# Dilated attention of the second block by head pairs, one step behind each half chunk of the input projection

## The reference, cut to what matters

```
proj = h @ w_in                                  # 512 x 1024 by 1024 x 3088 columns
mq, mk, mv, mo, mg, aq, ak, av = split(proj)
gates = mg + gate_bias
hm = bidirectional_mlstm(mq, mk * 64**-0.5, mv, gates...)     # 4 heads, both directions
hm = rms_norm(hm, g_mh) * sigmoid(mo)
qa = partial_rope(rms_norm(aq per head, g_q), pos) * 64**-0.5  # 8 heads of 64
ka = partial_rope(rms_norm(ak per head, g_k), pos)
ha = dilated_attention(qa, ka, av)               # three windows, dilations 1, 4, 16
return concat([hm, ha]) @ w_out
```

## Time and profile before

| | before |
|---|---|
| median of three runs | 3217.79 us |
| span of the profiled execution | 3213.4 us |
| TensorE busy | 3123.6 us, 97% |
| VectorE busy | 1911.2 us, 59% |
| ScalarE busy | 1046.4 us, 33% |
| mean granted TensorE clock | 0.985 |

### The profile page before, as it was taken

The page is one execution under the profiler, slowest core; times in us unless marked ns, Lnnn a source line. Parts: engine busy times, 40 slices in busy tenths (PEclk is TensorE's granted clock), DMA queues, the critical chain, the costliest instruction groups (busy, mean ns, idle before and its releaser), DMA issues.

```text
span 3213.4 us, 37101 instructions
## 1 busy us (share of the span) xinstructions
PE 3123.6 (97%) x15003; PEld 2512.4 (78%) x15014; DVE 1911.2 (59%) x2753; ACT 1046.4 (33%) x1516; POOL 10.2 (0%) x23
## 2 busy tenths in 40 slices
PE   8999999998899999999999999999999998899998
PEld 7888888776678888788877888788887764578887
DVE  7876555645675554766657554566665565574444
ACT  4212222335442222422235222332224444442222
POOL 0000000000000000000000000000000000000000
PEclk9999999999999999999999999999999999899999
DMA  6433332210033443256532443235551220133231
GB/s 231 141 118 127 147 126 81 68 46 11 2 132 127 158 153 131 79 192 214 196 107 79 150 158 138 79 118 202 185 189 59 78 59 1 47 119 104 92 99 53
DMA packets 102996, 369.21 MB, mean 115 GB/s; under 512 B 11374, under 2 KB 12670, under 8 KB 102572
## 3 DMA queue, kind: packets, MB, share of 16 engines
q1 hardware_dynamic: 101788, 362.14, 33.0%
q0 software_dynamic: 1040, 4.71, 0.4%
HBM read 364.71 MB, written 2.10 MB: 114 GB/s over the span
## 4 chain that ended last, share of the span: by engine, by line
PE 88%; DVE 7%; ACT 3%; issue 1%; DMA 1%; SPq 0%; POOL 0%; DVEq 0%; ACTq 0%; POOLq 0%
PE ps L192 25%; PE ps L194 25%; PE ps L193 25%; PE ps L196 4%; PE ps L197 2%; DVE SQ L614 1%; PE ps L499 1%; DVE WL L184 1%; DVE HL L603 1%; DVE XT L1037 1%; DVE RAW L1499 0%; PE ps L2888 0%; PE ps L2858 0%; PE ps L2788 0%; PE ps L2555 0%
## 5 line engine op out<-in xcount | busy, mean ns | idle before, releaser
L192 PE MATMUL ps<-HH,WH 128*128 128x512 f32 x2400 | 945.3, 394 | 4.0 <-ACT S L914 2.2
L194 PE MATMUL ps<-HH,WL 128*128 128x512 f32 x2400 | 935.1, 390 | 0.0
L193 PE MATMUL ps<-HL,WH 128*128 128x512 f32 x2400 | 934.5, 389 | 0.0
L179 ACT ACTIVATE WH<-RAW 128x1024 fp32r<-128x1024 f32 x456 | 459.2, 1048 | 632.0 <-PE ps L194 361.8
L184 DVE TENSOR_TENSOR WL<-RAW,WH 128x1024 fp32r<-128x1024 f32 x456 | 542.8, 1220 | 73.5 <-ACT WH L179 73.2
L192 PEld LDWEIGHTS ps<-HH,WH 128*128 128x128 f32 x2400 | 450.7, 188 | 107.5 <-issue 9.5
L193 PEld LDWEIGHTS ps<-HL,WH 128*128 128x128 f32 x2400 | 450.9, 188 | 95.2 <-issue 3.8
L194 PEld LDWEIGHTS ps<-HH,WL 128*128 128x128 f32 x2400 | 450.5, 188 | 95.4
L1037 DVE SCALAR_TENSOR_TENSOR XT<-ps,DER,XT 128x512 f32<-128x512 f32 x512 | 346.6, 683 | 246.6 <-PE ps L194 231.8
L192 PE MATMUL ps<-GH,WH 128*128 128x512 f32 x1056 | 414.1, 392 | 4.8 <-DVE GL L945 4.8
L194 PE MATMUL ps<-GH,WL 128*128 128x512 f32 x1056 | 411.2, 389 | 0.0
(11 more groups left out here) (382 smaller groups left out, 2627.0 us busy)
## 6 DMA issues: line engine op xcount, KB each, us to landing
RAW<-in_w_modt SPq DMA_DIRECT2D x200, 512.0 KB, 5.0
RAW<-in_ffn_wi SPq DMA_DIRECT2D x182, 512.0 KB, 5.0
RAW<-in_w_gu SPq DMA_DIRECT2D x90, 512.0 KB, 4.5
RAW<-in_ffn_wo SPq DMA_DIRECT2D x88, 512.0 KB, 4.6
RAW<-in_w_in SPq DMA_DIRECT2D x44, 512.0 KB, 3.6
RAW<-in_w_down SPq DMA_DIRECT2D x44, 512.0 KB, 4.2
RAW<-in_w_out SPq DMA_DIRECT2D x16, 512.0 KB, 4.5
STG<-in_w_modt SPq DMA_DIRECT2D x10, 512.0 KB, 12.7
```

The costliest lines, as they stand in the source:

```text
L179: act.e.activation(u.hi, u.ld.view, ACT.Copy).then_inc(u.hi_done.sem, 1)
L192: pe.e.matmul(out, wh, x[0], start=first, stop=False)
L193: pe.e.matmul(out, wh, x[1], start=False, stop=False)
L194: m = pe.e.matmul(out, wl, x[0], start=False, stop=last)
```

## The change

1. The alternation of units and attention is gone. `projection` takes a function `between`; a chunk's 24 matmuls are emitted as two halves, and the function is called after the first half and after the evacuation of the chunk. Each call takes one step of the attention.
2. The attention runs head pair by head pair: j outside, n inside. A pair now has two steps: the score of this pair and the first transpose group of the last one; then the second group, the value product of the pair before it, and the counts. A step waits in the list until the norm of its head pair has been emitted. The probabilities live in freed places of the weight ring.
3. The chunks are ordered DQ, DK, DV and one other, four times over, then MV, MQ, MK, MO. Chunks use banks 0 and 1, followers banks 2 and 3 (before: four each).
4. The norm is taken on 8 numbers per token: four matmuls with the square as the stationary operand and two columns of ones moving give a 128x8 sum; logarithm and exponential give the inverse root, three small VectorE operations refine it, and eight matmuls with a broadcast column spread it over the 64 partitions of its head. One part more per follower.
5. The eight spreads of the mLSTM's maxima move from the projection to the start of the mLSTM; the sigmoids of MO move from its evacuation to behind the last unit.
6. The quotient is written per head pair, and the high and low parts of chunks 4 to 7 are made beside the first units, not after the last quotient.

The core of the diff:

```
-            st["root"] = pr.sidefree[self.b] = s["nr_act"].next()
-            st["inv"] = s["rope"].next()
-            st["scaled"] = tiles.rsfree = s["rope"].next()
+            self.ln, st["root"] = s["nr_act"].next(), s["nr_act"].next()
+            self.prod, self.half, st["inv"] = (s["rope"].next() for _ in range(3))
+            pr.sidefree[self.b] = self.prod
...
-            pe.e.matmul(P.banks[self.b], ti.PR[:, 128:256], ti.SQ, start=True, stop=True).then_inc(st["sum"].sem, 1)
+            for n in range(4):
+                m = pe.e.matmul(P.banks[self.b][:, 2 * n:2 * n + 2], ti.SQ[:, n * 128:(n + 1) * 128], ti.PR[:, 128:256:64],
+                                start=True, stop=True)
+            m.then_inc(st["sum"].sem, 1)
         elif self.part == 2:
+            pe.wait_ge(*st["inv"])
+            pe.wait_ge(*self.free)
+            for n in range(4):
+                for h in range(2):
+                    rs = ti.RS[:, st["at"], 2 * n + h:2 * n + h + 1].broadcast_to([128, 64])
+                    m = pe.e.matmul(P.banks[self.b][64 * h:64 * h + 64, n * 128:(n + 1) * 128], rs, P.ID, start=True,
+                                    stop=True, skip_group_check=True)
...
-            act.e.activation(ti.RS, P.banks[self.b], ACT.Sqrt, scale=1.0 / 64, bias=P.EPSC).then_inc(st["root"].sem, 1)
+            act.e.activation(r, P.banks[self.b][:, 0:8], ACT.Ln, scale=1.0 / 64, bias=P.EPSC).then_inc(self.ln.sem, 1)
+            act.wait_ge(*self.ln)
+            act.e.activation(r, r, ACT.Exp, scale=-0.5).then_inc(st["root"].sem, 1)
...
+class MlSigmoid(Step):
...
+        for h in range(4):
+            act.e.activation(m.O[:, h, :], m.O[:, h, :], ACT.Sigmoid).then_inc(m.opened[h].sem, 1)
...
-        self.pairs = [(n, j) for n in range(4) for j in range(4)]
+        self.pairs = [(j, n) for j in range(4) for n in range(4)]
...
+                    if len(chs) == 1 and between:
+                        self.add(ProjMM(pr, [p], range(4)))
+                        between()
+                        self.add(ProjMM(pr, [p], range(4, 8)))
+                    elif len(chs) == 1:
                         self.add(ProjMM(pr, [p]))
                     if p.c0 == 0:
                         self.advance(lag)
                     evac(p)
+                    if len(chs) == 1 and between:
+                        between()
...
-                pr = Proj(self, h, (0, 1, 2, 3), (4, 5, 6, 7))
+                pr = Proj(self, h, (0, 1), (2, 3))
...
-                order = [DQ, DV, MG, DV + 1, DQ + 1, DV + 2, DV + 3, DQ + 2, MQ, MQ + 1, DQ + 3, MK, MK + 1]
                 for i in range(4):
-                    order += [DK + i, MV + i]
-                order += list(range(MO, MG))
+                    order += [DQ + i, DK + i, DV + i, MG if i == 0 else MV + i - 1]
+                order += [MV + 3, MQ, MQ + 1, MK, MK + 1] + list(range(MO, MG))
...
         split(0)
-        yield
+        done = [NONE] * 3
+        for h in range(4):
+            for d in range(2):
+                done.append(self.add(MlBroadcast(m, h, d, done[-3])).done)
+            if h % 2:
+                yield
...
     def dilated(self, w):
         last = len(w.pairs)
         for q in range(last + 2):
-            if 1 <= q <= last:
-                self.add(DilCount(w, q - 1))
             if q < last:
+                while w.pairs[q][0] not in w.qsplit or w.pairs[q][0] not in w.ksplit:
+                    yield
                 self.add(DilScore(w, q))
-                yield
             if 1 <= q <= last:
                 self.add(DilTrans(w, 2 * q - 2))
-                yield
+            yield
+            if 1 <= q <= last:
                 if q % 4 == 0:
                     self.add(DilDen(w, q // 4 - 1))
                 self.add(DilTrans(w, 2 * q - 1))
...
                 if q % 4 == 1:
                     self.add(DilQuot(w, q // 4 - 1))
-                yield
+            if q < last:
+                self.add(DilCount(w, q))
+            yield
+
+    def dilated_end(self, w, steps, mix):
+        for _ in steps:
+            yield
+        for k in range(4, 8):
+            self.add(MixSplit(self, mix, [k], [w.quot[k - 4].done]))
+            yield
```

More of the change, by code:

```diff
@@ L2261, in __init__ @@
         self.MKD = P.XT[:, 4, T:W].rearrange("p (d t) -> p d t", d=2)
-        room = lambda places: [P.over_ring(f"ROOM{i}{part}", [128, 2, T], F32, part + i * 4096)[:, half, :]
-                               for i in places for part in (0, NUNIT * 4096) for half in range(2)]
-        self.MB, kept = room(lent), room(kept)
+        kept = P.rooms(kept)
         self.NUM, self.MD = kept[0:8], kept[8:10]
@@ L2278, in tiles @@
         self.A = sb("A", [128, 4, T])
+        mb = sb("MB", [128, 8, T])
+        self.MB = [mb[:, i, :] for i in range(8)]
         self.RH = sb("RH", [36, T], F32R)
@@ L2414, with __init__ @@
 class MlBroadcast(Step):
[L2417 to L2422, removed]
+    def __init__(self, m, h, d, before):
+        self.m, self.h, self.d, self.b = m, h, d, (2 * h + d) % 3
+        self.split, self.free = m.mgsplit, before
+        self.spread = m.P.s["ml_mm"].next()
+        self.done = m.P.s["ml_act"].next()
         m.bcast[h, d] = self.done
@@ L2434, in scalar, with __init__ @@
     def scalar(self, act):
+        m, h = self.m, self.h
+        act.wait_ge(*self.spread)
+        act.e.activation(m.MB[self.d * 4 + self.h], m.P.banks[self.b], ACT.Copy).then_inc(self.done.sem, 1)
+class MlSigmoid(Step):
+    def __init__(self, m):
+        self.m = m
+        m.opened = [m.P.s["ml_gate"].next() for _ in range(4)]
+    def scalar(self, act):
         m = self.m
[L2436 to L2439, removed]
+        for h in range(4):
+            act.e.activation(m.O[:, h, :], m.O[:, h, :], ACT.Sigmoid).then_inc(m.opened[h].sem, 1)
 class MlMask(Step):
@@ L2772, in __init__ @@
         self.exp = [P.s["dil_exp"].next() for _ in range(2)]
-        self.bankfree = w.score[q - 1].exp if q else []
-        self.statfree = w.den[self.n - 2].spent if self.n > 1 else NONE
+        self.bankfree = w.score[q - 1].exp if q else [w.began]
+        self.statfree = w.den[self.j - 2].spent if self.j > 1 else NONE
         w.score[q] = self
@@ L3044, in at, with rooms @@
         return self.nc.alloc_sbuf_tensor_at(self.name(name), shape, dt, offset=address)
+    def rooms(self, places):
+        return [self.over_ring(f"ROOM{i}{part}", [128, 2, T], F32, part + i * 4096)[:, half, :]
+                for i in places for part in (0, NUNIT * 4096) for half in range(2)]
     def name(self, s):
@@ L3326, in follow, with projection @@
         lag.append(g)
-    def projection(self, pr, w, chunks, segs_of, evac, lag, beside=None, depth=1):
+    def projection(self, pr, w, chunks, segs_of, evac, lag, beside=None, depth=1, between=None):
         def job(chs):
```

178 lines of the change are left out of this document (101 added, 77 removed).

## The result

| | before | after |
|---|---|---|
| median, runs of one comparison | 3216.98 us (3214.17 to 3222.09, 17 runs) | 3223.93 us (3221.67 to 3229.55, 17 runs) |
| span of the profiled execution | 3213.4 us | 3221.7 us |
| TensorE busy | 3123.6 us | 3124.1 us |

The ratio is 1.0022, with a 95% interval of 1.0015 to 1.003: slower by 7 us, which is clear of the noise but small. The forecast was 3224 us.

What follows compares the result with a forecast made beforehand. TensorE bounds the projection (busy 163.15 of 164 us), while a chain of short VectorE and ScalarE steps makes the tail; +67.5 and -61.5 give +6, and 3213.4 + 6 + 4.4 gives 3224 us, range 3209 to 3238.

Steps and rivals of the forecast that it cites:

- pair in the projection: TensorE, projection: score 1.72, two transpose groups of 0.56 and value product 1.02, 3.86 us for each of 16 pairs.
- norm, each: TensorE, projection: two-column sums 0.7, spread 1.02 and 0.1 replace one 0.86 us matmul, +0.96 us, eight times.
- maxima spreads, eight: Projection: eight spreads leave, each holding TensorE about 0.85 us with its way back, -7 us.
- new waits in the projection: TensorE's queue, mainly second transposes waiting for ScalarE's bank 6 copy: 2 us in all, between 0 and 16.
- start and units with the first one's clock: mLSTM start 4.3 us later, units 3.0 us apart, value part ending 17 us earlier; half clock adds 1.5.
- tail: Last unit to first output matmul: chain without attention sums to 40.4 us against 88.3, -48, between -43 and -52.
- rival 1: Projection and tail: inserted steps cost only their streaming, pair under 3.5 us, tail frees 50; 3207 us, chance 0.20.
- the bounds 3.4 and 4.3: Projection: signs of being wrong, a pair at 3.4 us or below, or at 4.3 us or above.
- rival 2: Projection: scores, value products and norm spreads pay the maxima spreads' 0.4 us entry and exit, +12; 3236 us, chance 0.13.
- The margin: Projection: bank 6 copy takes 2.65 us under 3.15 us of cover, 0.5 spare; late by 0.2 to 0.7 behind a rotation.
- Rival 3: Projection: bank 6 or the maxima come 1 us late for every pair, +14 over the 2; 3238 us, chance 0.09.
- costs nothing now: Projection: VectorE's 3.35 us reciprocal, removed eight times, lay under TensorE's dense matmuls, so removal only makes room.

Runs made afterwards that it cites:

- the first step back: Kernel after with the last head pair's attention, from the step behind its first score on, left for the tail: 3219.23 us against 3217.68 for the kernel before.
- the next: Kernel after with the last two head pairs' eight attention steps left for the tail: 3223.41 us, 1.0021 of the kernel before.
- the wide norm: Kernel after with the norm on 128x512 by logarithm and exponential, refined one chunk later, no spread matmuls: 3236.98 us, 1.0066 of the kernel before.

## Why the prediction was right, point by point

| step | predicted us | measured us |
|---|---|---|
| pair in the projection | 3.86 | 3.92 (2.25 + 1.67) |
| quotient | 0.95 | 0.86 |
| norm, each | +0.96 | +1.11 |
| maxima spreads, eight | -7 | -6.9 |
| new waits in the projection | 2 | 0 |
| projection | +67.5 | +70.3 |
| start and units with the first one's clock | -15.5 | -15.8 |
| tail | -48 | -47.3 |
| clock of the output matmuls | +2 | +2.1 |
| sum | +6 | +9.3 (+8.3 in the span: the projection began 1.0 us earlier) |

- **Insertion (rival 1 false).** 3.92 us a pair is between the bounds 3.4 and 4.3 that were named. It is the price of a pair whose steps stand alone between dense matmuls; where a step stands beside a norm or a turn they share an entry, and the runs without attention give 64.8 us for all 16 pairs and four quotients, where 65.5 was forecast. A score alone has 0.1 us before it (2646.91 to 2647.23 is 0.32, where dense matmuls are 0.23 apart) and 0.1 behind it, which the 1.63 holds already (1.53 in the earlier trace rows). The Trainium skill says that changing the tiling mode drains TensorE (TensorEngine Tiling (Array Packing), Key Properties); the row agrees that the sides cost something, and puts it at 0.2 us for both sides of a score, not at the 0.4 of the maxima spreads, so rival 2 was false too. Whether it is the mode is open: the same 0.1 us stands behind the 128-row transposes (2606.42 to 2606.74 is 0.32), whose shape is that of the dense matmuls.
- **The norm** was under-sized: the group without a row, the sums of two columns, took 0.78 where 0.7 stood, and the spread 1.22 with its sides where 1.12 stood. Times eight, against the rounded +7 of the sum: 1.9 us.
- **Waits.** There were none for bank 6 in the kernel after, so the 2 us were too much. The margin, forecast at 0.5 us, and as missed by 0.2 to 0.7 behind a rotation, was 0.2 to 0.7 us and never negative: where the rotation's operations stood ahead of the maxima it was 0.22. Without the half chunk it turned into a wait of 2.1 us a pair, and with the old norm into up to 5.9 us. Rival 3 was the right danger. What kept it away is the norm on 8 numbers, which the prediction treated as a plain loss ("costs nothing now", "only makes room"). By the runs it costs 11 us alone, the move with the old norm costs 26 (3243.07 less 3217.32), and both together cost 7: the norm is what makes the move nearly free. The sum came out without this being seen: the prediction had the norm's price, and its waits were small for a reason that it named only in passing.
- **Table loads.** Between logarithm and exponential there is none. The kernel asks for the set that holds both (L2270), the projection's only load comes at 2472.71, and the eight pairs of logarithm and exponential and all of the attention's exponentials follow it without another. ScalarE's timeline after has the load and the first pair:

```profile
2472.71 1.28 ACT L2270 ACT_TABLE_LOAD   x1
...
2477.51 0.27 ACT L2229 ACTIVATE RS<-ps,K 128x8 f32<-128x8 f32 x1 [1.14 <-PE ps L2202]
2477.81 0.21 ACT L2231 ACTIVATE RS<-RS 128x8 f32<-128x8 f32 x1
```

The Trainium skill (ScalarE: Activation LUTs, Table sets: the hidden batching unit) says that one set has both, so that one load serves a logarithm and an exponential behind it; the trace agrees.
- **Start and units.** The first value product came 12.4 us after the projection (11.8 predicted, and "11 to 12" among the signs of being right, so a little late), units then 2.9 to 3.1 apart. The clock of the first unit cost 2.4 us, not 1.5.
- **Tail.** 41.6 us against 40.4. The single operations are close to those of the sum (heads 2.77 apart, inverses 4.6 in all); the squares ran at half clock (6.19 us for eight), which delayed the root by about 2 us.
- **The dense matmuls** were the one thing that no step contained: the last section.

That the time was hit to within 1 us is luck in two ways. The waits were too high by 2 us, the norm and the dense matmuls too low by 1.9 and 2.5, and the span came out 2.3 us above the forecast (+8.3 where +6 stood). And the 4.4 us between span and median, taken from the kernel before, were 2.2 after (3223.93 less 3221.7), which took these 2.3 back. The mechanism is not luck: the trade of two terms of 60 us stands by the runs without attention.

## What to carry to other kernels

Moving work from a stage in which TensorE waits into one in which it doesn't gains only the waits that it stood under: price the same work in both places (here 13.2 us in the tail against 18.4 in the projection for the first step back, 19.6 against 16.2 for the next), and look for the split, not for all or nothing. Count in the trace what an edit moved: the run meant to move four pairs moved three scores and two quotients. Before such a move, list the longest single instruction on each engine of the new place: a reciprocal of 3.3 us, free beside dense matmuls, made the move cost 26 us when a chain with some 0.5 us of margin stood behind it. Test an edit that looks like a loss together with the one it serves.

## What the hardware showed that was not expected

- Dense matmuls of the same shape were slower in the projection of every kernel that descends from the kernel after: mean distance of starts 0.2323 us against 0.2281 before, over more than 500 distances each; elsewhere in both kernels 0.227. Times 600 the difference of the projections is 2.5 us. It is not the attention (0.2325 without it), not the norm (0.2283 with the new norm in the kernel before, 0.23 and more with the old norm in the kernel after), not the half chunks (0.233 with whole ones) and not the order of the chunks (0.232 with another). What is left is that chunks take turns on two PSUM banks instead of four, or where tiles lie in SBUF; no run tells these apart. But the same distance (0.2328, mean of 179) stands in both kernels where dense matmuls read the tiles UH and UL, and these take turns on four banks; so two banks are not the only thing that can give it.
- Waits of TensorE in dense work were often, not always, followed by a stretch at half clock: four stretches behind the six waits with the old norm (one of 6.8 us, three of 3.4), four of 3.4 us behind the five of the wide norm, ten behind the sixteen with whole chunks.
- Eight instructions that move two columns each hold TensorE 0.78 us between dense matmuls, half as long as a whole score (1.63). Each brings a weight load of 128x128, and in the group at 2603.40 these loads cover 0.97 of its 0.98 us, so it is the load rather than the columns that seems to set the price here; no run takes the two apart.
